# Strassen's method, one level, in the first layer of two SwiGLU parts of a decoder layer

## The chip, the cores and the metric

One core of one Trainium2 chip runs the whole kernel; the other cores are idle. The metric is the device time of one execution in microseconds (us). Below, PE is TensorE, PEld its weight load, DVE is VectorE, ACT is ScalarE, POOL is GpSimd and SP is SyncE, here only a queue that issues DMAs. L852 is line 852 of the kernel.

## What is computed

One decoder layer for 512 prompt tokens and 8 x 4 sample tokens together (544 token columns), all in float32:

```
x = x + 0.5 * swiglu(rms_norm(x, g0), ffn_in[0], ffn_out[0])     # part 0
h = rms_norm(x, g1) @ w_in; three token mixers                   # sparse, dilated, pooling
x = x + mix @ w_out
x = x + 0.5 * swiglu(rms_norm(x, g2), ffn_in[1], ffn_out[1])     # part 1
def swiglu(h, w_io, w_o):
    gate, up = split(h @ w_io, 2)                                # 1024 -> 2 x 2816
    return (silu(gate) * up) @ w_o                               # 2816 -> 1024
```

The change is in the two feed-forward parts, which the code calls `ffn(0)` and `ffn(1)`.

## The kernel before

Activations lie transposed: features on the 128 partitions, tokens along the free axis, in two halves of 272 columns. Every float32 product is made of three matmuls of fp32r operands (`three`, L852 to L854): high x high, low x high, high x low. The high part of a weight or an activation is an ACT copy into fp32r (`lead` L1333 for weights, `parts` L1390 for the input), the low part is DVE's difference between the original and the high part (`remain` L1677, `hn` L1759).

Each part runs in two blocks of 11 feature tiles (`BCH`). For a tile of 128 gate and 128 up features, `chunk` on PE issues 2 halves x 2 (gate, up) x 8 slices of the contraction x 3 = 96 matmuls into four PSUM banks, the other four being the next tile's. ACT takes silu of the gate (L1405), DVE multiplies it by up (L1782), ACT makes the high part of this hidden row (L1409) and DVE the low part (L1772). After 11 tiles, `out_chunk` computes the 8 output tiles of the second layer from the 11 hidden rows, 66 matmuls each, and DVE adds them to x (L1801). Part 0 and part 1 have 2 x (11 x 96 + 8 x 66) = 3168 matmuls each.

SP loads the weights, one 128-column slice of 1024 rows (512 KB) per slot, into a ring of four slots; a slot is loaded again when PE has used it (`w_used`). POOL's queue only issues DMAs here: in part 0 the 33 copies of cache states to the outputs (L681), each waiting for a count of `w_used`.

Before the first tile of a part, `hn` on DVE makes the normalised input slice by slice, in turns with ACT, and PE starts with the first slice. In part 1, DVE first takes the reciprocal of the root (L1752). Each queue's order is written out in the code; semaphores join them.

## Time and profile before

| | us |
|---|---|
| three runs, lowest, median, highest | 1692.31, 1693.51, 1696.29 |
| profiled execution | 1691.56 |
| its span, first to last instruction | 1689.8 |
| PE busy in it | 1590.7 |
| DVE, ACT, POOL busy | 816.6, 656.8, 121.6 |
| part 1, first matmul to last | 1275.53 to 1678.28 |

An engine's busy time counts its instructions' durations, without issuing, semaphores and branches. Matmuls overlap: one of 272 columns is shown as 290 ns, though one starts every 125 ns. So PE's pace is read from counts per stretch of time. The span is 1.76 us shorter than the profiled execution's own time.

### The profile page before, as it was taken

How to read it: one execution, taken by the hardware profiler on the slowest of the kernel's cores; microseconds unless marked ns; L12 is line 12 of the kernel's file. 1: busy time of each engine (PE TensorE's matmuls, PEld its weight loads, DVE VectorE, ACT ScalarE, POOL GpSimd, SP SyncE). 2: the span in 40 equal slices, each digit the busy share in tenths (PEclk: the TensorE clock that was granted, in tenths of full speed). 3: DMA queues.
4: the chain of work that ended last, by engine and by line, in shares of the span. 5: the costliest groups of instructions: out<-in, count | busy, mean ns of one | idle time of the engine just before them, and what ended most of it. 6: DMA issues, size and time to landing. Idle time of an engine off the chain costs nothing.

```text
span 1689.8 us, 28006 instructions
## 1 busy us (share of the span) xinstructions
PE 1590.7 (94%) x11347; PEld 1478.7 (88%) x11347; DVE 816.6 (48%) x1527; ACT 656.8 (39%) x1172; POOL 121.6 (7%) x155
## 2 busy tenths in 40 slices
PE   4999998999999999999987998999798999999998
PEld 3778886999999999999976776777697999999998
DVE  4777779533433335436458995222356333233331
ACT  4556665322214332233335654555414342122221
POOL 0000000000000000001052002333000000000000
PEclk9999999999999999999977999999998999999999
DMA  8324230335434354242224005999122233232331
GB/s 314 117 107 193 100 124 27 124 125 186 157 117 149 124 174 140 88 154 90 79 77 129 1 1 143 255 258 260 49 88 63 76 98 103 71 88 77 106 90 66
DMA packets 183753, 202.27 MB, mean 120 GB/s; under 512 B 9894, under 2 KB 167309, under 8 KB 181069
## 3 DMA queue, kind: packets, MB, share of 16 engines
q1 hardware_dynamic: 167637, 111.67, 21.9%
q0 software_dynamic: 11680, 89.10, 15.5%
q10 hardware_dynamic: 4352, 0.34, 0.2%
q8 instruction: 58, 0.95, 0.2%
q14 instruction: 26, 0.21, 0.0%
HBM read 195.86 MB, written 31.40 MB: 134 GB/s over the span
## 4 chain that ended last, share of the span: by engine, by line
PE 84%; DVE 9%; ACT 3%; issue 2%; SPq 1%; DMA 1%; POOL 0%; ACTq 0%; DVEq 0%; PEldq 0%; POOLq 0%
PE PS L852 19%; PE PS L854 19%; PE PS L853 19%; PE PS L806 3%; PE PS L808 3%; PE PS L807 3%; PE PS L790 3%; PE PS L1209 2%; PE PS L1162 1%; PE PS L1137 1%; PE PS L1185 1%; SPq L595 1%; PE PS L1190 1%; ACT DEC L1531 1%; PE PS L1227 1%
## 5 line engine op out<-in xcount | busy, mean ns | idle before, releaser
L852 PE MATMUL PS<-HNH,WHI 128*128 128x272 f32 x1408 | 408.8, 290 | 7.6 <-DVE HNL L1759 6.7
L853 PE MATMUL PS<-HNL,WHI 128*128 128x272 f32 x1408 | 406.7, 289 | 0.0
L854 PE MATMUL PS<-HNH,WLO 128*128 128x272 f32 x1408 | 406.3, 289 | 0.0
L852 PEld LDWEIGHTS PS<-HNH,WHI 128*128 128x128 f32 x1408 | 267.1, 190 | 10.3 <-issue 7.8
L1333 ACT ACTIVATE WHI<-WR 128x1024 fp32r<-128x1024 f32 (+3 forms) x144 | 164.7, 1152 | 278.4 <-DMA WR<-in_ffn_in 128.9
L1677 DVE TENSOR_TENSOR WLO<-WR,WHI 128x1024 fp32r<-128x1024 f32 (+3 forms) x144 | 192.4, 1342 | 157.3 <-ACT WHI L1333 156.6
L853 PEld LDWEIGHTS PS<-HNL,WHI 128*128 128x128 f32 x1408 | 267.8, 190 | 0.0
L854 PEld LDWEIGHTS PS<-HNH,WLO 128*128 128x128 f32 x1408 | 267.6, 190 | 0.0
L1685 DVE TENSOR_TENSOR PT<-PS,PT 64x512 fp32r<-64x512 f32 x256 | 176.4, 689 | 66.3 <-ACT PT L1340 63.3
L852 PE MATMUL PS<-HIDH,WHI 128*128 128x272 f32 x704 | 202.4, 287 | 0.0
L854 PE MATMUL PS<-HIDH,WLO 128*128 128x272 f32 x704 | 202.4, 287 | 0.0
L853 PE MATMUL PS<-HIDL,WHI 128*128 128x272 f32 x704 | 201.9, 287 | 0.0
L1340 ACT ACTIVATE PT<-PS 64x512 fp32r<-64x512 f32 x256 | 151.8, 593 | 103.1 <-PE PS L790 101.5
L1782 DVE TENSOR_TENSOR BIG<-GB,PS 128x544 f32 (+1 forms) x44 | 31.7, 721 | 208.7 <-PE PS L854 207.0
L854 PEld LDWEIGHTS PS<-HIDH,WLO 128*128 128x128 f32 x704 | 132.5, 188 | 0.0
L853 PEld LDWEIGHTS PS<-HIDL,WHI 128*128 128x128 f32 x704 | 132.3, 188 | 0.0
L852 PEld LDWEIGHTS PS<-HIDH,WHI 128*128 128x128 f32 x704 | 132.0, 188 | 0.0
L806 PE MATMUL PS<-PT,CW1H 128*128 128x512 f32 x256 | 114.5, 447 | 2.6 <-DVE PT L1685 2.6
L807 PE MATMUL PS<-PT,CW1H 128*128 128x512 f32 x256 | 101.4, 396 | 0.0
L808 PE MATMUL PS<-PT,CW1L 128*128 128x512 f32 x256 | 101.4, 396 | 0.0
L1801 DVE SCALAR_TENSOR_TENSOR XT<-PS,XT 128x544 f32<-128x544 f32 x32 | 23.2, 724 | 158.6 <-PE PS L854 158.6
L852 PE MATMUL PS<-WHI,HNH 128*128 128x324 f32 (+1 forms) x256 | 80.3, 314 | 2.8 <-PE PS L961 2.8
(366 smaller groups left out, 2507.7 us busy)
## 6 DMA issues: line engine op xcount, KB each, us to landing
WR<-in_ffn_in SPq DMA_DIRECT2D x88, 512.0 KB, 3.7
WR<-in_ffn_out SPq DMA_DIRECT2D x32, 704.0 KB, 4.3
out_dil_s<-in_cache_dil_kv POOLq DMA_DIRECT2D x8, 2044.0 KB, 9.1
WR<-in_w_in SPq DMA_DIRECT2D x14, 648.0 KB, 4.3
BIG<-in_cache_dil_kv SPq DMA_DIRECT2D x8, 512.0 KB
WR<-in_w_out SPq DMA_DIRECT2D x8, 512.0 KB, 3.6
out_dil_s<-in_cache_dil_kv POOLq DMA_DIRECT2D x8, 508.0 KB, 5.0
out_win_s<-in_cache_win_kv POOLq DMA_DIRECT2D x8, 508.0 KB, 5.3
```

What stands on the lines that cost most here:

```text
L790: mm = pe.transpose(PS[:, 2 * (X % 2) + p, j * 256 + half * P:j * 256 + (half + 1) * P], PB[b % 2][:, half, c:c + P], ident)
L806: pe.matmul(out, hi, pt[:, 0, j, :, c:c + 256], start=(q == 0 and x == 0), stop=False)
L807: pe.matmul(out, hi, pt[:, 1, j, :, c:c + 256], start=False, stop=False)
L808: mm = pe.matmul(out, lo, pt[:, 0, j, :, c:c + 256], start=False, stop=(q == 3 and x == 3))
L852: pe.matmul(out, a[0], b[0], start=first, stop=False)
L853: pe.matmul(out, a[0], b[1], start=False, stop=False)
L854: return pe.matmul(out, a[1], b[0], start=False, stop=last)
L1209: mm = pe.matmul(out[:, t], ETA[0:R, j, :], kv[0:R, t, :, j * 256 + P:j * 256 + P + HD], start=(j == 0), stop=(j == 3))
L1333: act.activation(WHI[:, sl, 0:n], RAW[:, sl, 0:n], ACT.Copy).then_inc(w_hi, 1)
L1340: last = act.activation(PTX[X % 4][p * HD:(p + 1) * HD, 0, :, h, 0:256], PS[h * HD:(h + 1) * HD, 2 * (X % 2) + p, :].rearrange("p (j n) -> ...
L1677: V.tensor_tensor(WLO[:, sl, 0:n], RAW[:, sl, 0:n], WHI[:, sl, 0:n].bitcast(F32), ALU.subtract)\
L1685: last = V.tensor_tensor(pt[:, 1], src, pt[:, 0].bitcast(F32), ALU.subtract)
```

## The change

The first layer's product of a tile (256 features, 1024 contraction rows, 544 tokens) is cut in halves along all three: weights A11, A12 (gate) and A21, A22 (up), tokens and contraction B11 to B22. Strassen's method in Winograd's form makes it of seven products of 4 slices x 3 = 84 matmuls, one PSUM bank each, banks 0 to 6, with no second set for the next tile. Gate and up play the part of the two rows of the result.

- **Operands.** DVE forms four differences of input halves (T1 to T4) once per part; ACT and DVE make high and low parts of all seven (`operands`).
- **Weights.** POOL forms four sums of weight quarters per tile (`weight_sums`, 512 columns each). ACT and DVE make high and low parts of all seven, 512 columns each (`part_hi`, `part_lo`), in a ring of seven places.
- **Results.** ACT copies product B11 out of PSUM, DVE makes seven additions of 272 columns, each of a sum in SBUF and a product in PSUM; ACT takes silu of two sums, DVE multiplies them by two others. The low part of the hidden row goes from DVE to POOL (`hid_lo`).
- **Grouping.** The 22 tiles come in groups of 8, 7 and 7, each followed by the second layer over that group's hidden rows (8 output tiles).
- **Loads.** Four places of 512 KB; one is loaded again when DVE has made the last difference from it (`w_lo`), no longer when PE has used it.
- **State copies** of part 0 stand on POOL's queue between the weight sums.
- All loops are written out; on ACT the copies and silu share one loaded function table.

Core of the diff (a line of "..." marks what is left out; `operands` and `ffn` at the end are DVE's, the loop over `NSTEP` before `part_lo` is ACT's):

```diff
+GROUPS = ((0, 8), (8, 7), (15, 7))
+PART_SLOT = (2, 3, 4, 5, 6, 0, 1)
+PROD_B11, PROD_T1, PROD_T2, PROD_B22, PROD_T3, PROD_B21, PROD_T4 = range(7)
...
+        WP = put("WP", [P, 7, 2, 4 * P], "WR", 4 * 1024, dt=F32R)
+        WPF = WR[:, 4 * 1024:11 * 1024].rearrange("p (s x n) -> p s x n", s=7, x=2)
+        RAWF = WR[:, 0:4 * 1024].rearrange("p (s n) -> p s n", s=4)
...
+        def part_free(engine, f, q):
+            if q >= 7:
+                engine.wait_ge(w_used, Q_FFN[f] + q - 6)
+            elif f == 1:
+                engine.wait_ge(w_used, L_OUT + (6, 6, 7, 8, 8, 8, 8)[q])
+            elif q >= 2:
+                engine.wait_ge(m_done, NCH)
...
-                        sp.wait_ge(w_used, L + oc - RING + 1)
-                        sp.dma_start(RAW[:, sl, :].rearrange("p (k n) -> p k n", k=BCH),
-                                     src[:, :, oc * P:(oc + 1) * P]).then_inc(landed[sl], 16)
+                for in_layer1, first, n, x, q, u0 in STEPS:
+                    for u in range(u0, u0 + (2 if in_layer1 else 1)):
+                        if u >= 4:
+                            sp.wait_ge(w_lo, Q_FFN[f] + read[u - 4])
+                        elif f:
+                            sp.wait_ge(w_used, L_OUT + (5, 6, 7, 7)[u])
+                            sp.wait_ge(w_lo, L_OUT + 5 + u)
+                        if in_layer1:
+                            c = (first + x) * P + (u - u0) * FF
+                            sp.dma_start(RAWF[:, u % 4, :].rearrange("p (k n) -> p k n", k=KD), w1[:, :, c:c + P])\
...
+            def weight_sums(f, s):
+                _, _, _, _, q, u = STEPS[s]
+                done = 4 * tile_no(f, s)
+                raw_landed(pool, f, u)
+                raw_landed(pool, f, u + 1)
+                a11, a12, a21, a22 = (RAWF[:, (u + n // 2) % 4, n % 2 * 512:(n % 2 + 1) * 512] for n in range(4))
+                s1, s2, s4, s3 = (WPF[:, part_slot(q + j), 1, :] for j in (1, 2, 3, 4))
+                part_free(pool, f, q + 1)
+                nc.gpsimd.tensor_tensor(s1, a21, a22, ALU.add).then_inc(ff["weight_sums"], 1)
+                part_free(pool, f, q + 2)
+                pool.wait_ge(ff["weight_sums"], done + 1)
+                nc.gpsimd.tensor_tensor(s2, s1, a11, ALU.subtract).then_inc(ff["weight_sums"], 1)
+                part_free(pool, f, q + 3)
+                pool.wait_ge(ff["weight_sums"], done + 2)
+                nc.gpsimd.tensor_tensor(s4, a12, s2, ALU.subtract).then_inc(ff["weight_sums"], 1)
+                part_free(pool, f, q + 4)
+                nc.gpsimd.tensor_tensor(s3, a11, a21, ALU.subtract).then_inc(ff["weight_sums"], 1)
+            def hid_lo(f, s):
+                m = STEPS[s][3]
+                pool.wait_ge(ff["hid_hi"], tile_no(f, s) + 1)
+                nc.gpsimd.tensor_tensor(HIDL[:, m, :], HIDF[:, m, :], HIDH[:, m, :].bitcast(F32), ALU.subtract)                    .then_inc(ff["hid_lo"], 1)
...
+            for s, (in_layer1, _, _, x, q, _) in enumerate(STEPS):
+                if in_layer1:
+                    weight_sums(0, s)
+                if s and STEPS[s - 1][0]:
+                    hid_lo(0, s - 1)
+                while (in_layer1 or x < 4) and sent < N_COPIES and spread(pieces[sent][2]) < q + 7:
+                    pool.wait_ge(w_used, max(q, 1))
+                    pool.dma_start(pieces[sent][0], pieces[sent][1]).then_inc(cpy, 16)
+                    sent += 1
+            for n, (dst, src, before) in enumerate(pieces[sent:]):
+                pool.wait_ge(w_used, L_IN + min(12, 2 * n))
...
+                def product(s, j):
+                    q, t = STEPS[s][4] + j, tile_no(f, s)
+                    if s and STEPS[s - 1][0]:
+                        if j:
+                            pe.wait_ge(ff["partial"], 7 * (t - 1) + (0, 5, 1, 3, 4, 6, 7)[j])
+                        else:
+                            pe.wait_ge(ff["kept"], t)
+                    elif j in (0, 4):
...
+                    pe.wait_ge(w_hi, Q_FFN[f] + q + 1)
+                    pe.wait_ge(w_lo, Q_FFN[f] + q + 1)
+                    if s == 0:
+                        pe.wait_ge(r["hi"], j + 1)
+                        pe.wait_ge(r["lo"], j + 1)
+                    for k in range(4):
+                        mm = three(PS[:, j, 0:HALF], part(q, k), (TH[j][:, k, :], TL[j][:, k, :]), k == 0, k == 3)
+                    mm.then_inc(w_used, 1)
+                def features(s):
+                    _, first, n, oc, q, _ = STEPS[s]
+                    pe.wait_ge(bank_free[f], s + 1)
+                    if oc < 2:
+                        pe.wait_ge(ff["partial"], 7 * (FCH * f + first + n - 1) + 5 + oc)
+                    for j in range(2):
+                        pe.wait_ge(w_hi, Q_FFN[f] + q + j + 1)
...
+            def part_hi(f, q):
+                if q >= NQ:
+                    return
+                s = STEP_OF[q]
+                in_layer1, _, n, _, q0, u = STEPS[s]
+                j, sl = q - q0, part_slot(q)
+                if in_layer1 and 1 <= j <= 4:
+                    act.wait_ge(ff["weight_sums"], 4 * tile_no(f, s) + j)
+                    src = WPF[:, sl, 1, :]
+                elif in_layer1:
...
+                part_free(act, f, q)
+                act.activation(WP[:, sl, 0, 0:src.shape[-1]], src, ACT.Copy).then_inc(w_hi, 1)
...
+                for s in range(NSTEP):
+                    in_layer1, first, _, oc, q, _ = STEPS[s]
+                    t = tile_no(f, s)
+                    after_tile = s and STEPS[s - 1][0]
+                    if in_layer1:
+                        act.wait_ge(w_used, Q + q + 1)
+                        if t:
+                            act.wait_ge(ff["silu"], 2 * t)
+                        act.activation(SUM1, PS[:, 0, 0:HALF], ACT.Copy).then_inc(ff["kept"], 1)
+                        if after_tile:
+                            hid_hi(s - 1)
+                        for j in range(4):
+                            part_hi(f, q + j + 7)
+                        act.wait_ge(ff["partial"], 7 * t + 3)
+                        act.activation(GB[:, s % 2, 1, :], SUM3, ACT.Silu).then_inc(ff["silu"], 1)
+                        for j in (4, 5):
+                            part_hi(f, q + j + 7)
+                        act.wait_ge(ff["partial"], 7 * t + 6)
+                        act.activation(GB[:, s % 2, 0, :], SUM1, ACT.Silu).then_inc(ff["silu"], 1)
+                        part_hi(f, q + 6 + 7)
+                        continue
+                    if after_tile:
+                        hid_hi(s - 1)
+                    for j in range(2):
+                        part_hi(f, q + j + 7)
...
+            def part_lo(f, q):
+                if q >= NQ:
+                    return
+                s = STEP_OF[q]
+                in_layer1, _, n, _, q0, u = STEPS[s]
+                j, sl, w = q - q0, part_slot(q), 512
+                if in_layer1 and 1 <= j <= 4:
+                    if j <= 2:
+                        dve.wait_ge(ff["weight_sums"], 4 * tile_no(f, s) + j + 1)
+                    src = WPF[:, sl, 1, :]
+                elif in_layer1:
+                    src = RAWF[:, (u + (j == 6)) % 4, 0:512] if j == 0 else RAWF[:, (u + (j == 6)) % 4, 512:1024]
...
+                V.tensor_tensor(WP[:, sl, 1, 0:w], src, WP[:, sl, 0, 0:w].bitcast(F32), ALU.subtract).then_inc(w_lo, 1)
...
+                    if j:
+                        part_lo(f, j)
+                    dve.wait_ge(r["hi"], j + 1)
+                    V.tensor_tensor(TL[j][:, :, :], src, TH[j][:, :, :].bitcast(F32), ALU.subtract).then_inc(r["lo"], 1)
+                if f:
+                    dve.wait_ge(r["root"], 1)
+                    for hf in range(2):
+                        ins = V.reciprocal(RB[:, hf, :], RB[:, hf, :])
+                    link(ins)
+                for k in range(4):
+                    scaled(k)
+                sum_of(t1, b12, b11, 4)
+                rest(0, b11)
+                for k in range(4, 8):
+                    scaled(k)
+                sum_of(t2, b22, t1, 9)
+                rest(1, t1)
+                sum_of(t4, b21, t2, 10)
+                sum_of(t3, b22, b12, 10)
...
+                    if in_layer1:
+                        def add(n, out, a, bank, needs):
+                            if needs:
+                                dve.wait_ge(ff["partial"], 7 * t + needs)
+                            dve.wait_ge(w_used, Q + q + bank + 1)
+                            V.tensor_tensor(out, a, PS[:, bank, 0:HALF], ALU.add).then_inc(ff["partial"], 1)
+                        part_lo(f, q + 7)
+                        dve.wait_ge(ff["kept"], t + 1)
+                        add(1, SUM2, SUM1, PROD_T2, 0)
+                        add(2, SUM3, SUM2, PROD_T1, 1)
+                        add(3, SUM3, SUM3, PROD_B22, 2)
+                        part_lo(f, q + 8)
+                        add(4, SUM2, SUM2, PROD_T3, 0)
+                        add(5, SUM4, SUM2, PROD_T1, 4)
+                        for j in (2, 3, 4):
+                            part_lo(f, q + j + 7)
+                        add(6, SUM1, SUM1, PROD_B21, 0)
+                        add(7, SUM2, SUM2, PROD_T4, 0)
+                        dve.wait_ge(ff["silu"], 2 * t + 2)
+                        V.tensor_tensor(HIDF[:, x, HALF:T], GB[:, s % 2, 1, :], SUM4, ALU.mult)
+                        dve.wait_ge(ff["partial"], 7 * t + 7)
+                        V.tensor_tensor(HIDF[:, x, 0:HALF], GB[:, s % 2, 0, :], SUM2, ALU.mult).then_inc(bank_free[f], 1)
+                        part_lo(f, q + 12)
+                        part_lo(f, q + 13)
+                        continue
+                    oc = x
+                    part_lo(f, q + 7)
+                    if f == 0 and s == NSTEP - 1:
+                        remain(L_IN, KH * CG)
+                        remain(L_IN + 1, KH * CG)
...
```

PE, the first tile of part 0. Before, one product of eight contraction slices per bank (HNH and HNL are the input's high and low part, WHI and WLO the weight's; one slice of three stands here):

```order
L852 MATMUL PS<-HNH,WHI 128x272 [waits rms0_hi,rms0_lo,w_lo,w_hi]
L853 MATMUL PS<-HNL,WHI 128x272
L854 MATMUL PS<-HNH,WLO 128x272
L852 MATMUL PS<-HNH,WHI 128x272 [waits rms0_lo,rms0_hi]
L853 MATMUL PS<-HNL,WHI 128x272
L854 MATMUL PS<-HNH,WLO 128x272
```

And now (TH and TL are an operand's parts, WP the weight's; the first product's last slice and the second's first):

```order
L938 MATMUL PS<-TH_67,WP 128x272
L939 MATMUL PS<-TL_74,WP 128x272
L940 MATMUL PS<-TH_67,WP 128x272
L938 MATMUL PS<-TH_68,WP 128x272 [waits rms0_hi,rms0_lo,w_lo,w_hi]
L939 MATMUL PS<-TL_75,WP 128x272
L940 MATMUL PS<-TH_68,WP 128x272
```

A product now waits for one operand whole, four slices of 272 columns, where it waited slice by slice.

DVE, one pass of the loop over two tiles before (WLO is a weight's low part, BIG the hidden row, HIDL its low part; ISA and REGISTER_ALU rows belong to the loop):

```order
L1677 TENSOR_TENSOR WLO<-WR,WHI 128x1024 [waits w_hi]
L1676 REGISTER_ALU
L1677 TENSOR_TENSOR WLO<-WR,WHI 128x1024 [waits w_hi]
L1779 ISA
L1780 REGISTER_ALU [waits ffn0_silu]
L1782 ISA [waits w_used]
L1782 TENSOR_TENSOR BIG<-GB,PS 128x544
L1772 ISA [waits ffn0_hi]
L1772 TENSOR_TENSOR HIDL<-BIG,HIDH 128x544
```

And now, the third tile of part 0 (WP is a weight's low part, BIG and CKT the running sums, the two rows that read GB the hidden row's halves):

```order
L1937 TENSOR_TENSOR BIG<-BIG,PS 128x272 [waits w_used,ffn_kept]
L1937 TENSOR_TENSOR BIG<-BIG,PS 128x272 [waits w_used,ffn_partial] x2
L1813 TENSOR_TENSOR WP<-WR,WP 128x512 [waits w_hi,ffn_weight_sums]
L1937 TENSOR_TENSOR BIG<-BIG,PS 128x272 [waits w_used]
L1937 TENSOR_TENSOR CKT<-BIG,PS 128x272 [waits w_used,ffn_partial]
L1813 TENSOR_TENSOR WP<-WR,WP 128x512 [waits w_hi,ffn_weight_sums]
L1813 TENSOR_TENSOR WP<-WR,WP 128x512 [waits w_hi] x2
L1937 TENSOR_TENSOR BIG<-BIG,PS 128x272 [waits w_used] x2
L1956 TENSOR_TENSOR BIG<-GB,CKT 128x272 [waits ffn_silu]
L1958 TENSOR_TENSOR BIG<-GB,BIG 128x272 [waits ffn_partial]
L1813 TENSOR_TENSOR WP<-WR,WP 128x512 [waits w_hi] x3
```

Each weight is now differenced in seven pieces between the additions, most of which wait for a product (`w_used`); the first pieces wait for POOL's sums as well.

POOL, part 0 before: the whole of its queue in this part.

```order
L681 DMA out_dil_s<-in_cache_dil_kv 32x16352 [waits w_used] x8
L681 DMA out_dil_s<-in_cache_dil_kv 16x8128 [waits w_used] x8
L681 DMA out_win_s<-in_cache_win_kv 16x8128 [waits w_used] x8
L681 DMA out_dil_s<-in_cache_dil_kv 16x1984 [waits w_used] x8
L681 DMA out_pool_s<-in_state_pool 8x2816 [waits w_used]
```

And now, the third and fourth tile of part 0 (WR holds the weights, HIDL is the hidden row's low part):

```order
L732 TENSOR_TENSOR WR<-WR 128x512 [waits w_used,ring1_landed,ring0_landed]
L735 TENSOR_TENSOR WR<-WR 128x512 [waits ffn_weight_sums,w_used]
L738 TENSOR_TENSOR WR<-WR 128x512 [waits ffn_weight_sums,w_used]
L740 TENSOR_TENSOR WR<-WR 128x512 [waits w_used]
L745 TENSOR_TENSOR HIDL<-BIG,HIDH 128x544 [waits ffn_hid_hi]
L758 DMA out_dil_s<-in_cache_dil_kv 32x16352 [waits w_used]
L732 TENSOR_TENSOR WR<-WR 128x512 [waits w_used,ring3_landed,ring2_landed]
L735 TENSOR_TENSOR WR<-WR 128x512 [waits ffn_weight_sums,w_used]
L738 TENSOR_TENSOR WR<-WR 128x512 [waits ffn_weight_sums,w_used]
L740 TENSOR_TENSOR WR<-WR 128x512 [waits w_used]
L745 TENSOR_TENSOR HIDL<-BIG,HIDH 128x544 [waits ffn_hid_hi]
```

The difference of the tile before (L745) stands behind the sums for the next tile, and the copies stand among them.

## Rows read from the trace of the kernel before

**Rows 1.** The page: busy time of the engines, and the chain that ended last.

```profile
PE 1590.7 (94%) x11347; PEld 1478.7 (88%) x11347; DVE 816.6 (48%) x1527; ACT 656.8 (39%) x1172; POOL 121.6 (7%) x155
...
PE 84%; DVE 9%; ACT 3%; issue 2%; SPq 1%; DMA 1%; POOL 0%; ACTq 0%; DVEq 0%; PEldq 0%; POOLq 0%
```

**Rows 2.** Stretches: busy us (count) of PE, PEld, DVE, ACT, POOL, granted clock, DMA.

```profile
350.00:400.00 50.00, 50.00 (x400) 50.00 (x400) 16.43 (x17) 14.10 (x17) 1.02 (x2) 1.00 0.50 168
...
1400.00:1500.00 100.00, 100.00 (x800) 100.00 (x799) 29.75 (x28) 20.32 (x19) 0.00 (x0) 1.00 0.30 89
...
1272.00:1276.00 4.00, 0.47 (x2) 0.50 (x3) 3.83 (x6) 1.04 (x4) 0.00 (x0) 0.50 0.00 0
1276.00:1280.00 4.00, 4.00 (x18) 3.82 (x16) 3.96 (x11) 2.34 (x6) 0.00 (x0) 0.50 0.01 2
```

**Rows 3.** Waits in part 1: us in total, times, longest.

```profile
DVE BIG L1782 <- PE PS L854: 122.3, 21, 6.3
```

**Rows 4.** Timeline, start and end of part 1: start, duration, engine, instruction.

```profile
1272.05 1.85 DVE L1752 RECIPROCAL GB<-GB 128x272 f32<-128x272 f32 x1 [2.09 <-ACT GB L1358]
1275.53 0.57 PE L852 MATMUL PS<-HNH,WHI 128*128 128x272 f32 x1 [4.26 <-DVE HNL L1759]
...
1678.28 0.28 PE L854 MATMUL PS<-HIDH,WLO 128*128 128x272 f32 x1
```

**Rows 5.** DVE's groups by shape: count, busy us, mean ns, idle before.

```profile
L1677 DVE TENSOR_TENSOR WLO<-WR,WHI 128x1024 fp32r<-128x1024 f32 x96 | 116.7, 1224 | 81.7 <-ACT WHI L1333 81.1
L1759 DVE TENSOR_TENSOR HNL<-QTR,HNH 128x272 fp32r<-128x272 f32 x32 | 13.9, 435 | 0.9
L1815 DVE TENSOR_TENSOR HNL<-QTR,HNH 128x512 fp32r<-128x512 f32 x8 | 5.5, 686 | 0.0
```

**Rows 6.** ACT's groups by shape.

```profile
L1409 ACT ACTIVATE HIDH<-BIG x40 | 26.4, 660 | 117.1 <-DVE BIG L1782 117.1
L1390 ACT ACTIVATE HNH<-QTR 128x272 fp32r<-128x272 f32 x32 | 13.7, 431 | 17.8 <-DVE QTR L1755 17.8
L1428 ACT ACTIVATE HNH<-QTR 128x512 fp32r<-128x512 f32 x8 | 5.1, 633 | 49.4 <-DVE QTR L1809 49.4
```

**Rows 7.** Timeline of DVE, eight differences of 544 columns in a row.

```profile
1216.58 5.16 DVE L2191 TENSOR_TENSOR HNH<-HN,HNL 128x544 fp32r<-128x544 f32 x8
```

**Rows 8.** POOL's groups by shape.

```profile
L681 POOL DMA_DIRECT2D out_dil_s<-in_cache_dil_kv x24 | 11.8, 493 | 459.6 <-PE PS L854 427.9 <-PEq L968 31.7
L479 POOL TENSOR_TENSOR BIG<-BIG,WR 64x496 f32<-64x496 f32 x4 | 5.0, 1253 | 0.3
L465 POOL TENSOR_TENSOR BIG<-BIG 128x513 f32<-128x513 f32 x1 | 1.3, 1265 | 0.1
L465 POOL TENSOR_TENSOR BIG<-BIG 128x521 f32<-128x521 f32 x1 | 1.1, 1053 | 0.1
```

**Rows 9.** Timeline of POOL in the token mixer.

```profile
867.72 1.24 POOL L479 TENSOR_TENSOR BIG<-BIG,WR 64x496 f32<-64x496 f32 x1
869.04 1.05 POOL L465 TENSOR_TENSOR BIG<-BIG 128x521 f32<-128x521 f32 x1
...
875.05 1.02 POOL L478 TENSOR_TENSOR BIG<-BIG,CO 64x496 f32<-64x496 f32 x1
876.15 1.33 POOL L479 TENSOR_TENSOR BIG<-BIG,WR 64x496 f32<-64x496 f32 x1
```

**Rows 10.** Timeline of DVE beside it.

```profile
868.04 0.55 DVE L1949 TENSOR_TENSOR WR<-WR,PS 128x384 f32<-128x384 f32 x1 [3.75 <-PE PS L1023]
869.18 1.13 DVE L1952 TENSOR_TENSOR WR<-WR 128x192 f32<-128x192 f32 x1 [0.59 <-ACT WR L1481]
...
875.30 1.08 DVE L465 TENSOR_TENSOR BIG<-WR 128x288 f32<-128x288 f32 x1
```

**Rows 11.** DMA issues: count, KB each, median us from issue to landing.

```profile
WR<-in_ffn_in SPq DMA_DIRECT2D x88, 512.0 KB, 3.7
...
out_dil_s<-in_cache_dil_kv POOLq DMA_DIRECT2D x8, 2044.0 KB, 9.1
```

422 lines of the change are left out of this document (199 added, 223 removed).

## The prediction

> **What bounds the kernel now.** I read five views. The page's busy times show PE at 94% of the span, and the chain that ended last runs 84% over PE [rows 1]. The stretches inside the two feed-forward parts show PE without a gap, at the full 2.4 GHz (granted clock 1.00): 400 matmuls in 50 us, 800 in 100 us, so **0.125 us** for each matmul of 272 columns [rows 2]. The waits of the second part show DVE waiting for PE 122.3 us, and no wait of PE's for anyone comes near the list's top [rows 3]. The timeline gives this part's ends: reciprocal at 1272.05, first matmul at 1275.53, last at 1678.28 [rows 4]. With 3168 matmuls at 0.125 (396.0 us) inside 406.35 us, only 10.35 us are lost, all near the start, where the operands come one by one. So a matmul taken away is worth 0.125 us, as long as every other engine keeps up with a PE that is faster per tile.
>
> **What goes.** Strassen replaces the eight half-size products of a tile by seven: 7 x 4 x 3 = 84 matmuls instead of 96, the shape and the second layer unchanged. 44 tiles x 12 x 0.125 = **66.0 us less**, 33.0 in each part. A tile lasts 10.5 us instead of 12.0.
>
> **What comes, per tile.** DVE: seven differences of 512 columns, seven additions and two multiplications of 272. ACT: seven copies of 512, one of 544, three operations of 272. POOL: four sums of 512 and one difference of 544, which DVE had. Durations: DVE 0.69 us at 512, 0.43 at 272 [rows 5]; ACT 0.63, 0.43, 0.66 [rows 6]. Eight differences of 544 in a row take 5.16 us, so queued ones start 0.07 us sooner than their duration says [rows 7]. Busy time per tile: DVE 7 x 0.61 + 9 x 0.4 = 7.9 us, ACT 7 x 0.56 + 0.6 + 3 x 0.4 = 5.7 us, both under 10.5. By busy time alone the tile stays PE's.
>
> **POOL's price.** Nothing of POOL's runs here now except DMA issues of 0.49 us, so I take it from the token mixer. Two rows stand for it: 521 columns in 1.05 us, and 496 in 1.25 or 513 in 1.27 [rows 8]. The cheap one reads two places four columns apart; the dear ones read places further apart. The new sums read places at least 512 columns apart, so I take the dear rate: 512 columns 1.26 us, 544 columns 1.33 us; 1.04 and 1.09 are the other bound. The Trainium skill (GPSIMD Engine Reference, section 2.1, "Instruction dispatch") puts a two-input operation near 2.5 cycles per element at 1.2 GHz, an estimate of 1.07 us for 512 columns before the fixed part; that picks the dear row too, and with the cheap row the sum would be the first rival's.
>
> **The port.** While POOL works on SBUF, DVE operations with two SBUF inputs do not run beside it. Of 192 columns, one issued at 869.18 takes 1.13 us and ends 0.22 after POOL's; one of 288, issued at 875.30, takes 1.08 and ends 0.31 after POOL's [rows 9, 10]. The subtraction of 384 at 868.04 that reads PSUM takes its normal 0.55 us in the middle of a POOL operation [rows 10]. It works the other way too: POOL's operation at 876.15 takes 1.33 instead of the 1.24 at 867.72, while DVE's of 875.30 is still running. So DVE's differences and POOL's sums take turns, 1.1 ns per column (0.55 us for 512), while the additions from PSUM go free. The Trainium skill (SBUF — State Buffer, section "SBUF: two separate sides") has this as an exclusive lock held for the whole instruction, by which no pair of such operations overlaps anywhere; a shared bandwidth would give the second rival instead.
>
> **The loop.** Product T1 of the next tile waits for the fifth addition of this one, and this closes a circle over all queues. From a tile's last multiplication: ACT copy 0.71; POOL's 544 difference 1.38 + 0.33 behind a DVE difference; first weight sum 1.34 + 0.35; second 1.34 (each 1.26 and 0.08 between dependent ones [rows 9]); then, each queued behind a DVE difference that starts first, third and fourth 1.30 + 0.51 each (no wait on each other); ACT copy 0.68; DVE difference 0.65; sixth addition 0.48; silu 0.47; two multiplications 0.80. Sum **12.2 us** against PE's 10.5: a debt of 1.7 us a tile. Without the port's waits it is 10.5, with cheap sums 11.0. On DVE the weight parts of the next tile stand between the additions, so none of this can be overtaken.
>
> How many tiles pay: a group starts with its parts made in advance. Laid out tile by tile, the group of eight pays in tiles 4 to 8 (5 x 1.7 = 8.5 us), the groups of seven in the last three (0.6 + 1.7 + 1.7 = 4.0 each): **16.5 us** in each feed-forward part. Bounds: 0, and all 22 tiles, 37 us.
>
> **Into the second layer.** Each of three groups ends with the debt on display. PE waits 1.9 us for the fifth addition; the last hidden row then needs three differences, two additions, silu, multiplications, ACT's copy and POOL's difference, about 5.9 us, and PE has 33 matmuls (4.1 us) before it needs the row. 1.9 + 1.8 = 3.7 us, three times: **11.1 us** (bounds: 0.7 without debt, 20).
>
> **The start.** Seven operands must be made, by DVE, one product's worth at a time: in the second part two reciprocals (3.7), eight scalings of 544 (0.70 apart, 5.6), eleven operations of 1088 columns (1.22 apart, by the slope between the 512 and 1024 rows, 13.4), six weight differences (3.7), and the last product 1.65: the first tile ends 28.1 us after the reciprocal starts. POOL's sums for the second tile fall into it and block four differences by about 1.1 us and one by 0.4: 32.9. Minus 10.5 of matmuls, plus 0.4 in tile 2: 22.8 lost, 10.35 of which is lost today: **12.4 us more** (7.6 without the port).
>
> **Costed at nothing:** loads of 512 KB land after 3.7 us [rows 11]. SP's queue now issues them when DVE's differences are done, not when PE is; inside a group that is about 11 us before the first reader. Only at a change to the second layer is it 4 us, with ACT's copy and DVE's sixth addition queued behind the third load of the second layer: every us that it comes later is a us of PE's there. Silu's table reloads disappear, off the path. The second layer in three groups adds eight evacuations per part, hidden behind 5.2 to 6 us steps. In the first part POOL also issues the state copies (33 x 0.49 us, 2 MB ones 9.1 us in flight [rows 8, 11]) in front of its sums, and they fly beside the loads; I allow 4 us for that.
>
> **Sum.** Each part: -33.0 + 12.4 + 16.5 + 11.1 = +7.0; two parts +14.0, plus 4: **+18**. Against the profiled execution (1691.56 us, span 1689.8), 1709.5; that one lies 2 us under the median of 1693.51, so the median should be **1711 us**, 1% slower.
>
> **Rivals.**
> 1. Cheap POOL sums (1.04 us): loop 11.0, debt 0.5 a tile, first tile 32 us, transitions 2 to 3 us. The layout gives -29 us: 1665 us, and values between it and 1690 with a rate between. For: the 521-column row. Against: the 496 and 513 rows, nearer in kind.
> 2. No port conflict for these operations: 7.6 + 0.7 + 0 against 33.0, -25 each: 1644 us. Against: both blocked rows.
> 3. The loop binds all tiles, or loads come late as well: 22 x 1.7 = 37.4, so +28 each, 1745 us. It decides if loads land more than 11 us after their release, or if each queue's waits cost 0.1 us more than in today's rows: the loop has some fifteen of them, and the head start of a group is then spent two tiles earlier.
> 4. The costs cancel the gain: 1690 to 1697.
> 5. That it doesn't do what it says is excluded by the order: 2904 matmuls in each part instead of 3168.
> PE's clock stays in the width: it is 0.50 (1.2 GHz) from 1272 to 1280 us, after PE stood idle [rows 2]. The first tile's gaps may hold it there. Twelve matmuls at half speed, 3 us, keep DVE's pace of 2.9 us an operand, so this costs some 1.5 us on the last product and 1.5 in the tile behind it, at most 6 us over both parts.
>
> **Numbers.** Forecast (1697 to 1730) 0.46, the first rival 0.20, the second 0.08, the third 0.20, the fourth 0.06. A measurement can tell about 0.2% (3.4 us) from no change. Faster: 0.20 + 0.08 = 0.28; same 0.06; slower 0.66. Range 1665 to 1738: it takes in the first rival's end and most of the way to the third, and leaves out the second.
>
> **What would show it.** Right: PE's count down by 528; tiles near 12.2 us late in a group and 10.5 early, PE's idle time released by DVE's additions; POOL sums of 1.26 us alone and up to 1.8 behind DVE; DVE differences of up to 1.7 us; first tiles ending some 33 us after the reciprocal; PE idle 3 to 4 us at each change to the second layer. Wrong: POOL sums near 1.04 us with tiles under 11 us (first rival), or DVE differences that stay at 0.69 us beside POOL (second), or ACT waiting for loads in the tiles (third).

## The result, and the profile after

The changed kernel takes 1714.37 us (median of four, 1712.08 to 1723.09) against 1693.54 before; ratio **1.013**, 95% interval 1.0093 to 1.0168. It is slower, by 20.8 us; 1711 (1665 to 1738) was forecast. The profiled execution took 1714.78 us, its span is 1712.4 us, 22.6 longer than before.

The page, beside [rows 1]: PE's matmuls are 528 fewer, and a chain that was 84% PE is now 59%. What came in is DVE, POOL and "issue" (time in which an engine waited for nothing that the profile shows).

```profile
PE 1550.3 (91%) x10819; PEld 1424.4 (83%) x10819; DVE 1122.6 (66%) x2115; ACT 755.3 (44%) x1508; POOL 446.9 (26%) x375
...
PE 59%; DVE 13%; POOL 12%; issue 9%; ACT 4%; DMA 2%; SPq 1%; POOLq 0%; DVEq 0%; ACTq 0%; PEldq 0%
```

Stretches of the second feed-forward part, columns as in [rows 2]. Ahead of the first tile's end PE works half the time, on average at 0.63 of its clock; in the tiles it is full speed again (1.00) but idle 5.8 us of 82.9. In the tiles of [rows 2] it was never idle. No engine is full in the second stretch (PE busy 93% of it, DVE 85%, POOL 57%).

```profile
1289.50:1322.10 32.60, 16.78 (x85) 15.53 (x86) 32.35 (x31) 13.93 (x19) 7.21 (x4) 0.63 0.05 16
1322.10:1405.00 82.90, 77.12 (x590) 74.49 (x588) 70.69 (x116) 41.07 (x79) 47.34 (x31) 1.00 0.32 95
```

**One late tile.** POOL's timeline first, then DVE's beside it (start, duration, engine, instruction, idle time and who ended it). L732 to L740 are the four weight sums, L745 the hidden row's low part; on DVE, L1813 are weight differences, L1937 additions from PSUM, L1956 and L1958 the multiplications.

```profile
1381.08 1.71 POOL L738 TENSOR_TENSOR WR<-WR 128x512 f32<-128x512 f32 x1
1382.75 1.29 POOL L740 TENSOR_TENSOR WR<-WR 128x512 f32<-128x512 f32 x1
1388.21 1.65 POOL L745 TENSOR_TENSOR HIDL<-BIG,HIDH 128x544 fp32r<-128x544 f32 x1 [4.17 <-ACT HIDH L1507]
1389.83 1.75 POOL L732 TENSOR_TENSOR WR<-WR 128x512 f32<-128x512 f32 x1
1391.72 1.28 POOL L735 TENSOR_TENSOR WR<-WR 128x512 f32<-128x512 f32 x1
1393.15 1.71 POOL L738 TENSOR_TENSOR WR<-WR 128x512 f32<-128x512 f32 x1
```

```profile
1380.97 0.69 DVE L1813 TENSOR_TENSOR WP<-WR,WP 128x512 fp32r<-128x512 f32 x1 [1.33 <-POOL WR L735]
1381.58 0.43 DVE L1937 TENSOR_TENSOR BIG<-BIG,PS 128x272 f32<-128x272 f32 x1
1382.04 0.44 DVE L1937 TENSOR_TENSOR CKT<-BIG,PS 128x272 f32<-128x272 f32 x1
1382.82 2.97 DVE L1813 TENSOR_TENSOR WP<-WR,WP 128x512 fp32r<-128x512 f32 x3 [0.34 <-POOL WR L738]
...
1386.64 0.44 DVE L1956 TENSOR_TENSOR BIG<-GB,CKT 128x272 f32<-128x272 f32 x1
1387.00 0.43 DVE L1958 TENSOR_TENSOR BIG<-GB,BIG 128x272 f32<-128x272 f32 x1
1387.35 3.06 DVE L1813 TENSOR_TENSOR WP<-WR,WP 128x512 fp32r<-128x512 f32 x3
```

The third sum starts at 1381.08 and again at 1393.15: a tile lasts **12.07 us**, where PE needs 10.6. The loop of the prediction can be read off: multiplications done at 1387.4, ACT's copy of the row until 1388.1, POOL's 544 difference at 1388.21, then the sums one behind the other; POOL's own idle 4.17 us is the time it takes the circle to come round through ACT and DVE. A sum alone takes 1.28 or 1.29, behind a DVE difference 1.71 to 1.75. The additions at 1381.58 and 1382.04 read PSUM and keep their 0.43 and 0.44 us beside a running POOL sum, while three differences take 2.97 instead of some 1.9.

**The start of the part.** DVE's timeline, then POOL's. L1900 are operand differences of 1088 columns: 1.28 us, or 2.36 where a POOL sum for the second tile holds the port.

```profile
1310.40 1.28 DVE L1900 TENSOR_TENSOR TL<-BIG,TH 128x1088 fp32r<-128x1088 f32 x1
1311.60 0.68 DVE L1813 TENSOR_TENSOR WP<-WR,WP 128x512 fp32r<-128x512 f32 x1
1312.20 2.36 DVE L1900 TENSOR_TENSOR TL<-BIG,TH 128x1088 fp32r<-128x1088 f32 x1
```

```profile
1312.07 1.34 POOL L735 TENSOR_TENSOR WR<-WR 128x512 f32<-128x512 f32 x1 [2.15 <-PE PS L940]
```

**Into the second layer.** PE's timeline at a change of layers in the second part, then at the first one of part 0.

```profile
1405.29 0.37 PE L938 MATMUL PS<-HIDH,WP 128*128 128x272 f32 x1 [0.70 <-issue]
1411.17 0.36 PE L938 MATMUL PS<-HIDH,WP 128*128 128x272 f32 x1 [1.50 <-POOL HIDL L745]
```

```profile
416.25 0.56 PE L938 MATMUL PS<-HIDH,WP 128*128 128x272 f32 x1 [5.27 <-POOL HIDL L745]
```

Two short stops each time (0.7 to 0.9 and 1.7 to 1.8 us counted from matmul start to matmul start, above the usual distance), but 5.4 us for the second one at the first change in part 0. ACT's timeline tells why: its copy of a weight part waits 4.41 us for a load, and the hidden row's copy (L1507) stands behind it. The chain of waits has that load in flight for 11.05 us, not the 3.7 of [rows 11].

```profile
413.52 0.63 ACT L1437 ACTIVATE WP<-WR 128x512 fp32r<-128x512 f32 x1 [4.41 <-DMA WR<-in_ffn_out]
414.06 0.64 ACT L1507 ACTIVATE HIDH<-BIG 128x544 fp32r<-128x544 f32 x1
```

```profile
402.45 11.05 DMA WR<-in_ffn_out
```

That stop costs more than its own length. Behind it PE's granted clock is 0.50 (1.2 GHz) for 3.4 us, in which 15 matmuls run instead of the 27 or so of full speed; behind the 1.5 us stops of the second part it stays at 1.00. The stretch right after the stop:

```profile
416.20:419.60 3.40, 3.35 (x15) 3.38 (x16) 0.46 (x1) 0.00 (x0) 0.00 (x0) 0.50 0.73 214
```

**Where the time went.** From a part's first reciprocal to its last matmul, second part: 406.36 us before [rows 4], 411.53 now, +5.2. In part 0: 406.90 and 419.59, +12.7. Together +17.9. The other 4.7 us of the spans lie where the change touches nothing: 0.9 ahead of part 0 and 3.8 in the layers between the parts. Such stretches differ from kernel to kernel anyhow: the one from the token mixer's first reciprocal to that of part 1 alone lasts 399.9 us before, 402.8 here, and 399.8 to 402.8 in the kernels below.

### The profile page after: what moved, and what is told of

The parts are those of the page before. It is cut to its first block, busy times and chain, and to the rows that moved or that the text cites. A ratio compares the mean times of both kernels' runs of the same rounds, so it can differ in the third digit from the quotient of the medians.

```text
span 1712.4 us, 28054 instructions
## 1 busy us (share of the span) xinstructions
PE 1550.3 (91%) x10819; PEld 1424.4 (83%) x10819; DVE 1122.6 (66%) x2115; ACT 755.3 (44%) x1508; POOL 446.9 (26%) x375
## 4 chain that ended last, share of the span: by engine, by line
PE 59%; DVE 13%; POOL 12%; issue 9%; ACT 4%; DMA 2%; SPq 1%; POOLq 0%; DVEq 0%; ACTq 0%; PEldq 0%
PE PS L938 10%; PE PS L940 10%; PE PS L939 10%; PE PS L892 3%; PE PS L894 3%; PE PS L893 3%; PE PS L876 3%; POOL WR L738 3%; DVE WP L1813 3%; POOL WR L732 2%; POOL HIDL L745 2%; POOL WR L735 2%; PE PS L1293 2%; POOL WR L740 2%; PE PS L1221 1%
## 5 line engine op out<-in xcount | busy, mean ns | idle before, releaser
L1813 DVE TENSOR_TENSOR WP<-WR,WP 128x512 fp32r<-128x512 f32 (+1 forms) x404 | 351.3, 896 | 141.5 <-POOL WR L735 64.7
L938 PE MATMUL PS<-TH,WP 128*128 128x272 f32 x1232 | 364.7, 296 | 53.0 <-DVE TL L1900 30.6
L1437 ACT ACTIVATE WP<-WR 128x512 fp32r<-128x512 f32 (+1 forms) x404 | 243.1, 617 | 381.8 <-PE PS L940 133.8
L940 PE MATMUL PS<-TH,WP 128*128 128x272 f32 x1232 | 359.8, 292 | 0.0
L939 PE MATMUL PS<-TL,WP 128*128 128x272 f32 x1232 | 359.1, 291 | 0.0
L938 PEld LDWEIGHTS PS<-TH,WP 128*128 128x128 f32 x1232 | 235.6, 191 | 65.6 <-issue 39.1
L940 PEld LDWEIGHTS PS<-TH,WP 128*128 128x128 f32 x1232 | 236.0, 192 | 0.0
L939 PEld LDWEIGHTS PS<-TL,WP 128*128 128x128 f32 x1232 | 236.0, 192 | 0.0
L938 PE MATMUL PS<-HIDH,WP 128*128 128x272 f32 x704 | 204.3, 290 | 17.5 <-POOL HIDL L745 13.8
L940 PE MATMUL PS<-HIDH,WP 128*128 128x272 f32 x704 | 204.1, 290 | 0.0
L939 PE MATMUL PS<-HIDL,WP 128*128 128x272 f32 x704 | 203.4, 289 | 0.0
L938 PEld LDWEIGHTS PS<-HIDH,WP 128*128 128x128 f32 x704 | 133.2, 189 | 19.8 <-issue 19.8
L732 POOL TENSOR_TENSOR WR<-WR 128x512 f32<-128x512 f32 x44 | 68.5, 1556 | 280.8 <-PE PS L940 157.0
L939 PEld LDWEIGHTS PS<-HIDL,WP 128*128 128x128 f32 x704 | 133.3, 189 | 0.0
L940 PEld LDWEIGHTS PS<-HIDH,WP 128*128 128x128 f32 x704 | 133.1, 189 | 0.0
L745 POOL TENSOR_TENSOR HIDL<-BIG,HIDH 128x544 fp32r<-128x544 f32 x44 | 71.7, 1630 | 215.1 <-ACT HIDH L1507 215.1
L1937 DVE TENSOR_TENSOR BIG<-BIG,PS 128x272 f32<-128x272 f32 x264 | 110.1, 430 | 12.4 <-PE PS L940 9.7
```

The source lines that it names most:

```text
L745: nc.gpsimd.tensor_tensor(HIDL[:, m, :], HIDF[:, m, :], HIDH[:, m, :].bitcast(F32), ALU.subtract) .then_inc(ff["hid_lo"], 1)
L938: pe.matmul(out, a[0], b[0], start=first, stop=False)
L939: pe.matmul(out, a[0], b[1], start=False, stop=False)
L940: return pe.matmul(out, a[1], b[0], start=False, stop=last)
L1437: act.activation(WP[:, sl, 0, 0:src.shape[-1]], src, ACT.Copy).then_inc(w_hi, 1)
L1813: V.tensor_tensor(WP[:, sl, 1, 0:w], src, WP[:, sl, 0, 0:w].bitcast(F32), ALU.subtract).then_inc(w_lo, 1)
```

## The experiments

"Part 0" and "part 1" are the lengths of the feed-forward parts, as above; "first tile" is the time from the second part's reciprocal to the end of its seventh product (in before and b1 to the tile's last matmul); "pace" is the length of a late tile of part 1 on PE, without the stop at the change of layers. These four are from the traces. Each ratio is to the kernel before timed beside that run (medians 1692.1 to 1693.9).

| kernel | median us | ratio to before (95%) | part 0 | part 1 | first tile | pace |
|---|---|---|---|---|---|---|
| before | 1693.5 | | 406.9 | 406.4 | 20.6 | 12.06 |
| the change | 1714.4 | 1.0130 (1.0093 to 1.0168) | 419.6 | 411.5 | 32.6 | 12.07 |
| b1_seven_slices | 1630.4 | 0.9627 (0.9611 to 0.9643) | 374.8 | 373.9 | 20.2 | 10.5 |
| e1_hid_lo_later | 1728.7 | 1.0211 (1.0194 to 1.0228) | 424.0 | 422.7 | 32.6 | 12.9 |
| e2_near_inputs | 1683.3 | 0.9937 (0.9919 to 0.9955) | 411.5 | 394.0 | 31.6 | 10.6 to 11.1 |
| e3_no_sums | 1649.9 | 0.9751 (0.9735 to 0.9767) | 383.9 | 384.1 | 29.0 | 10.6 |
| e4_after_first_sum | 1691.4 | 0.9995 (0.9985 to 1.0004) | 407.8 | 401.3 | 32.6 | 10.6 to 11.9 |
| e5_distances (one run) | 1707.0 | | 415.1 | 406.8 | 31.6 | 10.6 to 12.1 |
| e6_copies_apart | 1708.8 | 1.0112 (1.0088 to 1.0136) | 415.1 | 411.6 | 32.5 | 12.1 |
| e7_hid_lo_dve | 1711.4 | 1.0114 (1.0094 to 1.0134) | 416.0 | 411.7 | 32.6 | 12.4 |
| e8_sum_and_copies | 1688.3 | 0.9963 (0.9949 to 0.9977) | 404.1 | 401.3 | 32.5 | 10.6 to 11.9 |
| e9_pairs | 1674.7 | 0.9875 (0.9855 to 0.9895) | 395.6 | 393.6 | 32.6 | 10.6 to 11.9 |

### b1_seven_slices: what a removed matmul is worth

```diff
 for k in range(KD):
     ...
+    if k == KD - 1:
+        continue
-    mm = three(..., k == 0, k == KD - 1)
+    mm = three(..., k == 0, k == KD - 2)
```

> The kernel before with one of eight contraction slices left out of the first layer's matmuls (84 instead of 96 a tile; that part of the product is not computed), all else as it was. If PE sets the pace and a matmul is worth 0.125 us wherever it goes: 44 x 12 x 0.125 = 66 us less, 1627 us. If something else takes over below 12 us a tile (loads, ACT, DVE of the kernel before): less gain, 1640 or more. This prices what Strassen removes, apart from all that it adds.

Measured: 1630.4, 62 to 63 us less; each part 32.1 to 32.5 us shorter. The gain that Strassen's method promises is there to be had. All of it and 21 us more go to what the change adds.

### e3_no_sums: POOL's sums taken out

```diff
-nc.gpsimd.tensor_tensor(s1, a21, a22, ALU.add).then_inc(ff["weight_sums"], 1)
+pool.sem_inc(ff["weight_sums"], 1)
...
-                    src = WPF[:, sl, 1, :]
+                    src = RAWF[:, u % 4, 0:512]
```

(and the same for the other three sums.)

> The change without POOL's four weight sums a tile (products T1, T2, B22 and T3 take a quarter of the weights in their place, so the result is not Strassen's); all waits and POOL's difference of 544 stay. If the sums' hold on the port and their place in the loop are what costs: every DVE difference 0.69 us, tiles of 10.5 us, first tile ending 28 to 29 us after the reciprocal, transitions under 1 us: 1645 to 1655. If the order of ACT's and DVE's queues binds by itself: tiles over 11 us and more than 1680.

Measured: 1649.9, 64 us less than the change. The pace is PE's, no stop over 0.3 us is left behind the first tile, and the first tile ends at 29.0. Stretches of this kernel inside the second part (columns as before):

```profile
1300.00:1340.00 40.00, 40.00 (x320) 40.00 (x319) 33.27 (x61) 22.16 (x42) 5.46 (x4) 1.00 0.34 99
1340.00:1400.00 60.00, 60.00 (x479) 60.00 (x479) 29.74 (x50) 18.43 (x32) 3.01 (x2) 1.00 0.32 94
```

DVE's timeline in it: three differences in a row take 1.89 us without a sum beside them, 2.97 in the change. The order of ACT's and DVE's queues does not bind by itself; the sums do. The run takes them off the port and out of the loop at once, so it does not say how the 64 us divide between the two.

```profile
1331.53 1.89 DVE L1813 TENSOR_TENSOR WP<-WR,WP 128x512 fp32r<-128x512 f32 x3
```

### e2_near_inputs and e5_distances: the price of a sum

```diff
+                near = RAWF[:, u % 4, 4:516]
...
-nc.gpsimd.tensor_tensor(s2, s1, a11, ALU.subtract)
+nc.gpsimd.tensor_tensor(s2, near, a11, ALU.subtract)
```

(all four sums; e5 has `dist:dist + 512` in place of `4:516`.)

> The change with all four POOL sums reading two places of the same weights four columns apart (so they compute something else, and the products that use them too), as the 521-column row of the token mixer does. If the distance of the two inputs sets POOL's price: sums of 1.04 us alone instead of 1.28, late tiles near 11.1 us instead of 12.05, 1675 to 1690. If something else makes that row cheap: 1.28 stays and the time stays at 1714.

Measured: 1683.3, 31 us less than the change. POOL's groups in the second part: the two sums that mostly run alone average 1.07 and 1.09 us; the other two still wait for DVE.

```profile
L741 POOL TENSOR_TENSOR WR<-WR 128x512 f32<-128x512 f32 x22 | 23.9, 1086 | 5.2 <-PE PS L941 5.2
L736 POOL TENSOR_TENSOR WR<-WR 128x512 f32<-128x512 f32 x22 | 23.5, 1066 | 8.2 <-PE PS L941 5.9
```

So a quarter of a microsecond per sum is worth 31 us in the kernel. This is the prediction's first rival made real: the loop of 11.1 us is the 11.0 that it gave, but the time is 18 us above its 1665. Much of that lies in part 0, which is only 8 us shorter than in the change, where part 1 is 17.5 shorter: at its second change of layers PE now stops for 7.6 us. ACT waits there for a load that takes 12.8 us beside a 2 MB copy:

```profile
538.37 0.63 ACT L1438 ACTIVATE WP<-WR 128x512 fp32r<-128x512 f32 x1 [6.40 <-DMA WR<-in_ffn_out]
```

> A measurement inside the change: all four POOL sums of a tile read two places of the same weights (their results are no Strassen sums), and the distance between the two grows from tile to tile: 0, 1, 2, 4, 8, 12, 16, 24, 32, 48, 64, 96, 128, 192, 256, 384, 512 columns, then 4, 64, 256, 512, 4. If distance sets the price: 1.04 to 1.07 us up to some distance and 1.27 above, with a step. If another thing made e2_near_inputs cheap (one operand less from a different tile, or no sum read right after it was written): 1.07 at every distance.

POOL's timeline of e5, the second sum (L738) at distances of 4, 8, 64 and again 4 columns:

```profile
343.71 1.04 POOL L738 TENSOR_TENSOR WR<-WR 128x512 f32<-128x512 f32 x1
355.03 1.29 POOL L738 TENSOR_TENSOR WR<-WR 128x512 f32<-128x512 f32 x1
472.19 1.30 POOL L738 TENSOR_TENSOR WR<-WR 128x512 f32<-128x512 f32 x1
599.14 1.04 POOL L738 TENSOR_TENSOR WR<-WR 128x512 f32<-128x512 f32 x1
```

It is a step: undisturbed sums take 1.04 us at 0, 2 and 4 columns, 1.28 to 1.31 at each of the 13 distances from 8 to 512 (the one tile with distance 1 lies in the busy start of a part and tells nothing; 3 and 5 to 7 were not run). The sums of e5 differ in nothing but the distance, so the second theory falls. The choice of the dear row of [rows 8] was right, and for the reason given with it; the two rows of L465 there are one line of the kernel at distances 4 (521 columns, 1.05 us) and 8 (513 columns, 1.27), so they lie on the two sides of this step.

### e1_hid_lo_later: the order of POOL's queue, first try

```diff
+            def late_hid_lo(f, s):
+                if s >= 2 and STEPS[s - 2][0] and STEPS[s - 1][0]:
+                    hid_lo(f, s - 2)
+                if s and STEPS[s - 1][0] and not STEPS[s][0]:
+                    hid_lo(f, s - 1)
...
-                if s and STEPS[s - 1][0]:
-                    hid_lo(1, s - 1)
+                late_hid_lo(1, s)
```

(the same in part 0.)

> The change with POOL's queue in another order: a tile's low part of the hidden row comes after the next tile's four weight sums instead of ahead of them. Theory A, a loop of dependencies in which POOL's difference delays the sums (12.05 us a tile): the loop is cut, tiles fall to PE's 10.5 us, 33 us less over both parts and some at the transitions, 1675 to 1680. Theory B, the shared port is itself full: seven weight differences of 0.61 and two multiplications of 0.37 on DVE plus 4 x 1.28 + 1.35 on POOL are 11.5 us a tile, whatever the order: tiles of 11.5, 1690 to 1702.

Measured: 1728.7, 14 us more than the change. **Both theories fall.** POOL's timeline, then DVE's:

```profile
1382.73 1.29 POOL L732 TENSOR_TENSOR WR<-WR 128x512 f32<-128x512 f32 x1 [5.26 <-PE PS L943]
1384.17 1.31 POOL L735 TENSOR_TENSOR WR<-WR 128x512 f32<-128x512 f32 x1
1385.65 1.29 POOL L738 TENSOR_TENSOR WR<-WR 128x512 f32<-128x512 f32 x1 [0.18 <-PE PS L943]
...
1388.61 1.79 POOL L745 TENSOR_TENSOR HIDL<-BIG,HIDH 128x544 fp32r<-128x544 f32 x1
```

```profile
1383.38 0.94 DVE L1959 TENSOR_TENSOR BIG<-GB,CKT 128x272 f32<-128x272 f32 x1 [0.15 <-ACT GB L1530]
1384.25 1.53 DVE L1961 TENSOR_TENSOR BIG<-GB,BIG 128x272 f32<-128x272 f32 x1
1385.70 5.26 DVE L1816 TENSOR_TENSOR WP<-WR,WP 128x512 fp32r<-128x512 f32 x3
```

The tiles last 12.9 us. POOL is free when PE releases the first place, so its five operations run in a row, from 1382.73 to 1390.40, each ahead of DVE. That is just when DVE has its two multiplications (0.94 and 1.53 instead of 0.44) and three differences queued (5.26 us, against 1.89 without sums). The additions that PE waits for stand behind them. Cutting the loop at POOL hands the loop to DVE, which is now busy, its blocked time counted in, 12.64 of the 12.9 us of a tile. The sum of theory B, 11.5 us, is below the measured tile, so what counts is not the sum of time on the port but who is on it when DVE has two-input work in front of an addition.

### e4_after_first_sum: the order of POOL's queue, second try

```diff
                 part_free(pool, f, q + 1)
                 nc.gpsimd.tensor_tensor(s1, a21, a22, ALU.add).then_inc(ff["weight_sums"], 1)
+                if s >= 2 and STEPS[s - 1][0] and STEPS[s - 2][0]:
+                    hid_lo(f, s - 2)
                 part_free(pool, f, q + 2)
```

(the last two rows of a group are made in its first step of the second layer.)

> The change with POOL's difference of the hidden row between the first and the second weight sum of the tile after next (in the change it stands ahead of the first, in e1_hid_lo_later behind the fourth). Theory A (the loop and the port together: what counts is which of POOL's operations run while DVE has two-input work queued): the first sum then runs during DVE's additions from PSUM, which it does not disturb, so the loop is 1.34 us shorter and nothing of DVE's is blocked more: tiles of 10.6 to 10.9 us, 1668 to 1685. Theory B (e1's lesson is that every move of the difference behind a sum lets POOL block DVE's multiplications): 12.5 us a tile or more, 1720.

Measured: 1691.4, no difference from before (0.9995, 0.9985 to 1.0004) and **23 us less than the change**, from one operation's place in one queue. In the group of eight of part 1 the last three tiles last 11.6 to 11.9 us, with PE's two stops down from 1.3 us together to between 0.8 and 1.0; in the groups of seven the fourth lasts 11.3 and the later ones 10.6 to 10.8, near PE's own pace. At the second change of layers in part 0 PE stops for 4.2 us (2.4 in the change). POOL's timeline in a tile of the group of eight, then DVE's:

```profile
1354.17 1.28 POOL L732 TENSOR_TENSOR WR<-WR 128x512 f32<-128x512 f32 x1 [0.43 <-PE PS L944]
1359.01 1.65 POOL L747 TENSOR_TENSOR HIDL<-BIG,HIDH 128x544 fp32r<-128x544 f32 x1 [3.56 <-ACT HIDH L1511]
1360.62 1.74 POOL L737 TENSOR_TENSOR WR<-WR 128x512 f32<-128x512 f32 x1
```

```profile
1352.53 4.08 DVE L1817 TENSOR_TENSOR WP<-WR,WP 128x512 fp32r<-128x512 f32 x3 [0.35 <-POOL WR L740]
...
1357.81 0.44 DVE L1962 TENSOR_TENSOR BIG<-GB,BIG 128x272 f32<-128x272 f32 x1
1358.16 3.05 DVE L1817 TENSOR_TENSOR WP<-WR,WP 128x512 fp32r<-128x512 f32 x3
```

The first sum has moved into the time in which POOL stood idle in the change, and is done (1355.45) before the multiplications, which keep their 0.44 us; the circle behind the hidden row is one sum shorter. Theory A is right on the loop and wrong on the port, and its 1668 to 1685 is missed by 6 us: the early sum falls in this tile on none of the additions, but on DVE's three differences, which now take 4.08 us, two of them blocked, instead of 2.97. So part of the gain is given back on the port. Another part goes to the 4.2 us stop, which e8 takes up.

### e7_hid_lo_dve: POOL's difference back on DVE

```diff
                         part_lo(f, q + 13)
+                        dve.wait_ge(ff["hid_hi"], t + 1)
+                        V.tensor_tensor(HIDL[:, x, :], HIDF[:, x, :], HIDH[:, x, :].bitcast(F32), ALU.subtract)\
+                            .then_inc(ff["hid_lo"], 1)
```

> The change with the hidden row's low part made by DVE (544 columns, 0.72 us), as before the change, behind the tile's seven weight differences; POOL keeps only the sums. If POOL's hop in the loop is what costs: 1.6 us out of the loop and 1.4 us less on the port, tiles of 10.5 to 11, 1680. If DVE's own queue takes its place (its seven differences, nine short operations and this one, three of them blocked by sums): tiles near 12.1 us as now, but transitions 2 us shorter each because the last row is done sooner: about 1704.

Measured: 1711.4, 3 us less than the change, within its interval. A tile lasts 12.4 us, and in the second part the stops at the changes of layers shrink from 1.7 to 0.65 us, as the second theory has it; its time of 1704 is missed by 7 us, with a pace forecast 0.3 us too low. The trace shows what it left out, and it is what e1 showed. POOL has no difference to wait for any more and makes its four sums in a row from 1385.66, just when DVE has its multiplications:

```profile
1385.66 1.30 POOL L732 TENSOR_TENSOR WR<-WR 128x512 f32<-128x512 f32 x1 [6.50 <-PE PS L936]
```

```profile
1386.31 0.94 DVE L1952 TENSOR_TENSOR BIG<-GB,CKT 128x272 f32<-128x272 f32 x1
1387.18 1.53 DVE L1954 TENSOR_TENSOR BIG<-GB,BIG 128x272 f32<-128x272 f32 x1
```

The same 0.94 and 1.53 us as in e1. DVE is busy 12.15 us of this tile's 12.4, and its own hidden-row difference stands ahead of the next additions.

### e6_copies_apart: the load that came late

```diff
-                while (in_layer1 or x < 4) and sent < N_COPIES and spread(pieces[sent][2]) < q + 7:
+                while (x < 4) and sent < N_COPIES and spread(pieces[sent][2]) < q + 7:
```

(`x` counts from 0, so the first four tiles of a group and the first four output tiles send copies.)

> The change with no state copy issued during tiles 5 and later of a group (they wait for the next second layer). If the 5.4 us stop at the first change of layers in part 0 comes from a load that shares the DMA engines with a 2 MB copy: that stop shrinks to the 1.7 us of the other transitions, 4 us less, 1710. If it comes from the order of POOL's queue or from anything else, the stop stays.

Measured: 1708.8, 5.6 us less by the medians (the intervals of the two ratios overlap, so the trace has to decide). Part 0 is 4.5 us shorter and part 1 the same. PE's stop at the first change of layers is now

```profile
411.82 0.36 PE L938 MATMUL PS<-HIDH,WP 128*128 128x272 f32 x1 [1.50 <-POOL HIDL L745]
```

1.50 as in the second part, where no copies run, not 5.27. The load that took 11.05 us takes 5.4 here, and ACT no longer waits for it; so it was the 2 MB copy beside it. A copy still slows the loads beside it (one beside two copies now takes 17 us), but none of PE's stops hangs on those.

Taken apart by stretches, part 0 is 5.2 us shorter at the first change of layers and 1.1 in the last group's tiles, which have no copies in POOL's queue now. It is 1.8 longer at the second change: PE's stop there is 2.9 us (2.4 in the change) behind a load of 5.8 us with no 2 MB copy in flight, and the granted clock is 0.50 for 3.4 us behind it. Why that load is slow stays open.

### e8_sum_and_copies and e9_pairs: a version that beats both

> e4_after_first_sum and e6_copies_apart together. If the 4.2 us stop of e4 at a change of layers in part 0 is the one that e6 removed: about 3 to 5 us less than e4, 1687. If the two share nothing: 1691 as e4.

Measured: 1688.3, 0.9963 (0.9949 to 0.9977): part 0 is 3.7 us shorter than in e4, part 1 the same. The 4.2 us stop is 2.4 now. It is the first kernel here that computes the whole layer by Strassen's method and is faster than the one before.

e9 changes what PE does first in the second layer:

```diff
+                    if oc == 0:
+                        pe.wait_ge(bank_free[f], s + 1)
+                        pe.wait_ge(ff["kept"], FCH * f + first + n)
+                        contract(s, 0, q)
+                        pe.wait_ge(ff["partial"], 7 * (FCH * f + first + n - 1) + 6)
+                        contract(s + 1, 0, q + 1)
+                        contract(s, 1, q + 2)
+                        contract(s + 1, 1, q + 3)
```

(`contract(s, j, p)` is the half j of an output tile's contraction with weight part p; ACT, DVE and the loads follow the new order of parts. The first output tile also goes to banks 0 and 7, so that it need not wait for the fifth addition. The two were not run apart.)

> e8 with another order at each change to the second layer: the first two output tiles take the first four hidden rows, then both the rest, so PE has 6.9 to 7.1 us of matmuls ahead of the last hidden row instead of 4.1; the first one uses banks 0 and 7, so it does not wait for the fifth addition. If the two stops there (0.8 and 1.7 us, six times) are the debt of the last row, nearly all of it is covered: 13 to 15 us less than e8, 1672. If the row gets later with it (DVE's or ACT's queue behind something that the new order delays): 5 us or less.

Measured: **1674.7**, ratio to before 0.9875 (0.9855 to 0.9895), 13.6 us less than e8. None of the six stops at a change of layers is over 0.3 us any more (part 1: 7.8 us shorter). It is 1.2% faster than before and 2.3% faster than the change. In the group of eight the last three tiles still last 11.6 to 11.9 us, with the loop of e4. Behind that group PE's 279.00 busy us in 280 show that little is left there:

```profile
1268.00:1301.00 33.00, 15.12 (x89) 13.86 (x90) 32.79 (x32) 14.24 (x19) 8.35 (x4) 0.73 0.07 19
...
1380.00:1660.00 280.00, 279.00 (x2211) 278.17 (x2211) 188.94 (x299) 105.85 (x199) 107.36 (x71) 1.00 0.30 87
```

Of the 44 us that remain between 1674.7 and b1's 1630.4 more than half, 2 x 12.4, is the longer start (32.6 us to the end of the first tile against 20.2), which the first row shows: DVE busy 32.79 of 33 us with the operands while PE waits. No kernel here tried to shorten it.

## Why the prediction was right, step by step

Second part, by its own terms (stops are distances between matmul starts, above the usual one):

| term | forecast | measured |
|---|---|---|
| matmuls gone | -33.0 | -32.6 (b1: -32.5) |
| start | +12.4 | +13.5 |
| loop, late tiles | +16.5 | +16.6 |
| changes of layers | +11.1 | +7.6 |
| second part | +7.0 | +5.2 |
| part 0 | +7.0 and 4 | +12.7 |
| both | +18 | +17.9 |

- **What goes**: right. The gap between matmuls is 0.1256 us before and 0.1258 now, so 264 fewer are worth 32.6 with the change of pace.
- **POOL's price**: right, 1.28 to 1.30 us against 1.26 taken; e5 gives the reason, the distance of the inputs. The Trainium skill's figure (GPSIMD Engine Reference, section 2.1), 1.07 us before the fixed part, is near e2's 1.04 to 1.07, not near these sums. The measurement decides.
- **The port**: right, in both directions (2.36 us for a difference of 1088 columns instead of 1.28; sums of 1.71 behind a difference; additions from PSUM untouched), and e3 shows what the sums cost through port and loop together: 64 us. What the prediction did not draw from it is what e1 and e7 show: which operation comes first decides who waits. The Trainium skill has that rule (SBUF — State Buffer, "Who interferes with whom": issue order, not the shape of the operation, decides who blocks), and e1's rows agree: five POOL operations in a row, each ahead of a DVE operation that then takes 0.94 to 1.8 us.
- **The loop**: right, 12.07 against 12.2. In the group of eight PE stops once in tile 3 and twice in each of tiles 4 to 8, in a group of seven from tile 5 on. The layout had all but the tile 3, which lasts 11.2 us; the last three tiles of a group of seven cost 1.0, 1.5 and 1.5 us against 0.6, 1.7 and 1.7. 13.9 of the 16.6 us are stops in which two matmuls start over 0.29 us apart.
- **Into the second layer**: mechanism right, **size wrong**: some 0.8 and 1.7 us each time, not 1.9 and 1.8. The term took the fifth addition to come as late in a group's last tile as in the others; but then POOL has no sums of a next tile to make, DVE is not blocked, and the last row is done some 3 us sooner after its predecessor (8.9 to 9.1 us between the last two copies of hidden rows of a group, not 12.07).
- **The start**: first tile's end forecast 32.9, measured 32.55, with four differences blocked by 1.1 us each, as laid out. The term is 1.1 too small all the same, because the kernel before loses 8.5 us in its start by its real gap of 0.1256, not 10.35. PE's clock, left in the width at up to 6 us, cost next to nothing there: it is 0.50 until 1313.9, but 1.00 for the last three products, and the second tile lasts 10.8 us.
- **Costed at nothing**: the loads. The wait was named (ACT's copy and the row behind it), but 4 us were allowed in part 0 where 7.5 were lost: 5.4 instead of 1.7 at one change of layers, 2.4 instead of 1.8 at the next, and two tiles of 12.6 us near the end. The trace puts 5.3 us at the first change of layers (3.8 for the longer stop and 1.5 for the half clock behind it, which the prediction did not have), 1.3 in those tiles, 0.6 at the second change and the rest in small pieces. e6 gives 4.5 of the 7.5 back.
- **Rivals**: the first is what e2 made; the second is excluded by every blocked row (e3 does not speak to it, because it leaves the sums out); the third did not happen in part 1, where no load is waited for in a tile. The third's price is also summed wrongly: twice 28 us above before is 1749, not 1745. Both lie outside the range.

The mechanism was right; that the sum came so close is partly luck. In the second part the changes of layers came out 3.5 us lower and the start 1.1 higher than forecast, 1.8 lower in all, and part 0 came out 1.7 higher. The profiled execution is 5 us above its forecast of 1709.5, nearly all of it in the 4.7 us outside the two parts, where nothing was forecast and where the kernels with the change differ by 3 us among themselves.

## What to carry to other kernels

A step can be bound with no engine full: in the late tiles of the change PE, DVE and POOL all had idle time, and still a tile lasted 1.5 us longer than PE's work. After taking work from the busiest engine, add up the circle of dependencies through all queues, not each engine's busy time. Where two engines share a port, look at what the other has in front of the critical operation at that moment; moving one POOL operation back by one place gained 23 us, moving it back by four places lost 14. And a debt that shows only at the end of a group can be paid with work that does not need the late row: 13.6 us from the order of four half contractions and the banks of the first.

## What the runs showed of the hardware that was not expected

GpSimd's operation with two inputs in SBUF was cheaper where they lay 0, 2 or 4 fp32 columns (up to 16 bytes) apart: 1.04 us for 512 columns in e5, and 1.28 to 1.31 from 8 columns on, without a further step up to 512. The Trainium skill (SBUF — State Buffer, "Door 1: The DMA port swizzle") speaks of lines of 16 bytes and a penalty for each access that crosses to a new one; the step between 4 and 8 columns fits that, but no run here shows that it is the cause. A weight load in flight beside a 2 MB copy took 11.05 us in the change, 5.4 in e6 without the copy, and 12.8 in e2 beside another one; the median of such loads in the change is 4.2 to 4.5. And behind PE's stop of 5.3 us the granted clock was 0.50 for 3.4 us, worth 1.5 us more.
